# Last block: two chunks of the gated unit ahead of the last readout, and eight smaller moves on TensorE, ScalarE and VectorE

## The reference, cut to what matters

```python
def second_block(x, p, mix_norm, w_in, ...):
    xn = rms_norm_2(h, mix_norm[i])
    z = xn @ w_in[i]
    q, k, v, gate_a, u, gate_s = jnp.split(z, splits, axis=-1)
    attn = dilated_mixture_attention(q, k, v, ...) * jax.nn.silu(gate_a)
    ssm = s5_glu(u, ...) * jax.nn.silu(gate_s)
    h = h + jnp.concatenate([attn, ssm], axis=-1) @ w_out[i]
    gate = jax.nn.sigmoid(rms_norm_2(h, ple_norm[i]) @ w_ple_gate[i])
    h = h + gate * (p[i] @ w_ple_proj[i])
```

## Time and profile before

| what | value |
|---|---|
| median of 3 runs | 1368.23 us (1367.81 to 1368.30) |
| the profiled execution, its own time | 1368.63 us |
| its span, first to last instruction | 1366.9 us |
| mean granted TensorE clock | 0.999 |
| TensorE matmul busy | 1344.7 us (98%) |
| VectorE busy | 1020.6 us (75%) |
| ScalarE busy | 791.3 us (58%) |
| chain that ended last | TensorE 84%, VectorE 11%, ScalarE 3% |

### The profile page before, as it was taken

The page is one execution under the profiler, slowest core; times in us unless marked ns, Lnnn a source line. Parts: engine busy times, 40 slices in busy tenths (PEclk is TensorE's granted clock), DMA queues, the critical chain, the costliest instruction groups (busy, mean ns, idle before and its releaser), DMA issues.

```text
span 1366.9 us, 20597 instructions
## 1 busy us (share of the span) xinstructions
PE 1344.7 (98%) x6811; PEld 1105.3 (81%) x6811; DVE 1020.6 (75%) x1930; ACT 791.3 (58%) x1546; POOL 177.0 (13%) x323
## 2 busy tenths in 40 slices
PE   7999999999999999999999999999999999999998
PEld 6888888889987888889888888888888888887657
DVE  6978666669666766669766666699887777889986
ACT  6676555456555645558656554567665555675444
POOL 4100000000111000002000000001049993000000
PEclk9999999999999999999999999999999999999999
DMA  8534767775533767783336677745356766554132
GB/s 282 166 124 128 241 215 217 220 240 184 162 103 113 245 217 216 229 253 110 124 96 220 215 223 232 244 147 177 124 173 216 226 223 230 169 175 131 66 123 93
DMA packets 180310, 249.24 MB, mean 182 GB/s; under 512 B 10393, under 2 KB 124641, under 8 KB 180241
## 3 DMA queue, kind: packets, MB, share of 16 engines
q1 hardware_dynamic: 152352, 224.05, 50.7%
q10 hardware_dynamic: 25920, 18.89, 4.6%
q0 software_dynamic: 1968, 5.43, 1.4%
HBM read 237.84 MB, written 10.49 MB: 182 GB/s over the span
## 4 chain that ended last, share of the span: by engine, by line
PE 84%; DVE 11%; ACT 3%; issue 1%; DMA 1%; ACTq 0%; SPq 0%; DVEq 0%
PE ps L2112 21%; PE ps L2114 21%; PE ps L2113 21%; DVE w_rest L1382 3%; PE ps L2118 3%; PE ps L2126 3%; PE ps L2122 3%; ACT w_head L830 1%; PE ps L2448 1%; DVE x L1445 1%; PE ps L2933 1%; PE ps L2934 1%; PE ps L2935 1%; PE ps L2142 1%; PE ps L2965 1%
## 5 line engine op out<-in xcount | busy, mean ns | idle before, releaser
L2112 PE MATMUL ps<-w_head,xt_head 128*128 128x512 f32 (+1 forms) x1152 | 448.0, 389 | 3.3 <-DVE w_rest L1382 2.9
L2114 PE MATMUL ps<-w_head,xt_rest 128*128 128x512 f32 (+1 forms) x1152 | 441.5, 383 | 0.0
L2113 PE MATMUL ps<-w_rest,xt_head 128*128 128x512 f32 (+1 forms) x1152 | 441.0, 383 | 0.0
L830 ACT ACTIVATE w_head<-w_raw,gain_t 128x512 fp32r<-128x512 f32 (+1 forms) x596 | 375.1, 699 | 84.3 <-PE ps L2114 24.1
L1382 DVE SCALAR_TENSOR_TENSOR w_rest<-w_raw,gain_t,w_head 128x512 fp32r<-128x512 f32 (+1 forms) x596 | 417.3, 764 | 5.4 <-ACT w_head L830 4.7
L2112 PEld LDWEIGHTS ps<-w_head,xt_head 128*128 128x128 f32 x1152 | 217.2, 189 | 48.3 <-issue 6.4
L2114 PEld LDWEIGHTS ps<-w_head,xt_rest 128*128 128x128 f32 x1152 | 217.1, 188 | 42.9
L2113 PEld LDWEIGHTS ps<-w_rest,xt_head 128*128 128x128 f32 x1152 | 217.4, 189 | 39.8
L830 ACT ACTIVATE w_head<-w_raw 128x1024 fp32r<-128x1024 f32 x124 | 124.6, 1053 | 80.2 <-PE ps L2114 76.7
L1380 DVE TENSOR_TENSOR w_rest<-w_raw,w_head 128x1024 fp32r<-128x1024 f32 x124 | 146.8, 1222 | 6.6 <-ACT w_head L830 6.2
L1990 DVE SCALAR_TENSOR_TENSOR hid<-ps,rstd_x,gate_s 128x256 f32<-128x256 f32 x88 | 38.6, 480 | 119.3 <-ACT gate_s L1126 119.3
(11 more groups left out here) (502 smaller groups left out, 1699.1 us busy)
## 6 DMA issues: line engine op xcount, KB each, us to landing
w_raw<-in_ffn_w_gate_dram SPq DMA_DIRECT2D x88, 512.0 KB, 4.3
w_raw<-in_ffn_w_up_dram SPq DMA_DIRECT2D x88, 512.0 KB, 5.9
w_raw<-in_ffn_w_down_dram SPq DMA_DIRECT2D x88, 512.0 KB, 6.2
w_raw<-in_a_w_in_dram SPq DMA_DIRECT2D x48, 512.0 KB, 4.7
w_raw<-in_b_w_in_dram SPq DMA_DIRECT2D x24, 512.0 KB, 4.7
w_raw<-in_w_in_dram SPq DMA_DIRECT2D x24, 512.0 KB, 4.7
hid_way<-q_t ACTq DMA_DIRECT2D x36, 256.0 KB, 2.0
k_t<-hid_way ACTq DMA_DIRECT2D x144, 64.0 KB, 5.0
```

Source lines behind the costliest of these rows:

```text
L830: ins = act.activation(w_head[:, s, w], raw(u)[:, w], ACT.Copy, scale=1.0 if by is None else by)
L2112: pe.matmul(out_, hd, wh, start=first, stop=False)
L2113: pe.matmul(out_, hd, wr, start=False, stop=False)
L2114: return pe.matmul(out_, rt, wh, start=False, stop=last)
```

## The change

No instruction is added or taken out, and no operand changes. On TensorE, `half_unit(11, 1)` goes ahead of `readout(1)`; `weights_turned(2)` and `scores(3)` go ahead of `driven(6)` and `o_turn(0)`, and `readout(2)` ahead of `values(2)`; `o_turn(1)` goes between the two `out_a(1, (0, 1), m)`; and `glu(0)` and `glu(1)` go ahead of `readout(3)`. On ScalarE, `spread_out(1)` goes ahead of `proj_copied(0)` and `turned(gs_t[:, 0:2, :], 7)`, `spread_out(2)` ahead of `turned(gs_t[:, 2:4, :], 7)`, `head(u + OUT_S)` ahead of `gelu(3)`, and the second half of `head(u + OUT_S + 1)` behind the last `ssm_copied`. On VectorE, `gated(3)` goes into the middle of `turned_out(6)`. SyncE's and GpSimd's programs keep their order.

```diff
--- before.py
+++ after.py
@@ -1275,13 +1275,13 @@
                 spread_out(0)
                 exp(1)
                 out_of(5, gs_d, ACT.Silu)
+                spread_out(1)
                 proj_copied(0)
                 turned(gs_t[:, 0:2, :], 7)
-                spread_out(1)
                 exp(2)
                 proj_copied(1)
+                spread_out(2)
                 turned(gs_t[:, 2:4, :], 7)
-                spread_out(2)
                 o_copied(0)
                 exp(3)
                 spread_out(3)
@@ -1290,9 +1290,9 @@
                 gelu(1)
                 gelu(2)
                 o_copied(1)
+                head(u + OUT_S)
                 gelu(3)
-                head(u + OUT_S)
-                head(u + OUT_S + 1)
+                head(u + OUT_S + 1, some=(0, 2))
                 gate(0)
                 gate(1)
                 ssm_copied(0)
@@ -1301,6 +1301,7 @@
                 gate(3)
                 ssm_copied(2)
                 ssm_copied(3)
+                head(u + OUT_S + 1, some=(2, 4))
                 u += OUT_S + 2
                 n["x"] += 4
                 n["bank"] += 2
@@ -1607,7 +1608,7 @@
                     dve.wait_ge(bu_taken, h + 1)
                     step(dve.tensor_tensor(z1, z1, t_, ALU.subtract))
 
-                def turned_out(h):
+                def turned_out(h, between=None):
                     g, half = h // 2, h % 2
                     cs, sn = half_tiles(g, half)
                     t_, z0, z1, e_ = s5_piece[h]
@@ -1618,6 +1619,8 @@
                     step(last)
                     dve.tensor_tensor(t_, z0, cs, ALU.mult)
                     step(dve.scalar_tensor_tensor(e_, z1, -1.0, sn, ALU.mult, ALU.mult))
+                    if between:
+                        between()
                     dve.tensor_tensor(z0, z0, sn, ALU.mult)
                     dve.tensor_tensor(z1, z1, cs, ALU.mult).then_inc(xs_done, 1)
 
@@ -1698,8 +1701,7 @@
                 turned_in(6)
                 gated(2)
                 y_out(2)
-                turned_out(6)
-                gated(3)
+                turned_out(6, lambda: gated(3))
                 turned_in(7)
                 ssm_part(0)
                 turned_out(7)
@@ -2532,8 +2534,8 @@
                 pe.wait_ge(in_out, 8)
                 pe.wait_ge(turn_used, tr + 7)
                 values(0)
+                half_unit(11, 1)
                 readout(1)
-                half_unit(11, 1)
                 weights_turned(1)
                 pe.wait_ge(in_out, 12)
                 project(0)
@@ -2547,15 +2549,15 @@
                 project(1).then_inc(unit_used, 1)
                 pe.wait_ge(o_done_v, n["o_v"] + 2)
                 turn_group(gs_d, 1, 7)
+                weights_turned(2)
                 driven(6)
-                weights_turned(2)
+                pe.wait_ge(t_done, pair + 3)
+                scores(3)
                 pe.wait_ge(turn_used, tr + 9)
                 o_turn(0)
-                pe.wait_ge(t_done, pair + 3)
-                scores(3)
+                readout(2)
                 pe.wait_ge(o_there, 1)
                 values(2)
-                readout(2)
                 weights_turned(3)
                 pe.wait_ge(proj_out, 2 * M)
                 for m in range(M):
@@ -2563,9 +2565,9 @@
                 driven(7)
                 pe.wait_ge(o_done_v, n["o_v"] + 3)
                 values(3)
-                for m in range(M):
-                    out_a(1, (0, 1), m)
+                out_a(1, (0, 1), 0)
                 o_turn(1)
+                out_a(1, (0, 1), 1)
                 pe.wait_ge(o_there, 2)
                 for m in range(M):
                     last = out_a(0, (2, 3), m)
@@ -2574,10 +2576,11 @@
                     last = out_a(1, (2, 3), m)
                 last.then_inc(unit_used, 1)
                 pe.wait_ge(bu_taken, 8)
+                glu(0)
+                glu(1)
                 readout(3)
-                for k in range(4):
-                    last = glu(k)
-                last.then_inc(unit_used, 1)
+                glu(2)
+                glu(3).then_inc(unit_used, 1)
                 out_s_both(0)
                 there, base = xs(), n["xt"]
```

## The result

The median of 17 runs is 1372.43 us (1368.62 to 1374.35), against 1368.23 (1367.70 to 1368.70) before. The ratio is 1.0028, with a 95% interval of 1.0021 to 1.0034: slower by 4.2 us, 1.5 us above the end of the range. What the median hides is that the 17 executions are of two kinds. Before, all lay within 1.0 us. Now five have a mean granted TensorE clock of 1.000 and take 1368.62 to 1370.51, mean 1369.4. The other twelve have 0.996 to 0.998 and take 1371.77 to 1374.35, mean 1373.1. The profiled execution is of the second kind: 1373.14, span 1371.4, clock 0.996.

A forecast was written before the change was run, and what follows sets the result against it. TensorE, busy 98% of the span, was taken to bound the kernel. Waits going (3.0 us) against waits coming (4.4) and a tail count of 1.1 to 1.2 more gave 1369.4 us, range 1367.0 to 1370.9.

The forecast's parts named there:

- The chain of lateness: `readout(1)` behind the half unit delays VectorE 1.8 us at `turned_in(4)`; TensorE then waits 2.1 before `gs_d`'s second transpose.
- The wait for `exp(2)`: Before `weights_turned(2)` on TensorE: 0.7 us more of waiting, the transpose ending at 1293.1 against `exp(2)` at 1293.8.
- ScalarE's heads: Before `gelu(3)`: cost nothing while their loads are there; 0.3 to 0.4 us late at the longest landing, 0.4 kept for range.
- TensorE through the middle: From `project(0)` to the first `out_a`: new waits of 2.1 and 0.7 us, `out_a` starting at 1302.0, 1.4 late.
- rival (c): TensorE's clock falls during the new waits of 2.1 and 0.7; twelve slower matmuls cost 2.3 us, 1371.7; chance 0.07.
- (a): VectorE's delay does not reach TensorE; the 2.1 falls to 0.25 and only the tail is paid: 1367.5 us; chance 0.13.
- (b): Every wait of TensorE goes and none comes, the tail's included: -3.0, or 1365.2 us; chance 0.05.
- (d): `gated(3)` misses `o_turn(1)`, so VectorE's 1.8 comes through whole: 1370.1 us; chance 0.75 together with the forecast.
- the points that should prove the prediction wrong: No VectorE gap at `turned_in(4)`; `rest` ending before the first gate; 512-column matmuls behind the new waits starting over 0.4 apart.
- twelve matmuls near the start: After idling on loads in the earlier trace they took 5.20 us, 0.43 each, against 0.24 in a half unit.

The follow-up runs named there:

- the wait filled: The change with the second half of `project(1)` multiplied twice, four matmuls more before the second transpose of `gs_d`: 1369.21 us.
- the two variants that keep those waits: The change with `readout(3)` back ahead of all four `glu` chunks, 1372.54 us; the kernel before's change with only `rest(u + OUT_S)` moved ahead of `y_out(3)`, 1372.09 us.
- `glu` back: The change with `readout(3)` back ahead of all four chunks of the gated unit, the other moves kept: 1372.54 us, ratio 1.0027 to before.
- the longer wait: The kernel before with `half_unit(11, 1)` ahead of `readout(1)`, and the second transpose of `gs_d` also waiting for `exp(2)`: 1373.43 us.

## Why the prediction was wrong, point by point

**What held.** The chain of lateness came as it was worked out. VectorE stood still 1.87 before `turned_in(4)` (1.8 forecast), TensorE 1.97 before the transpose (2.1), 0.9 before `project(0)` (0.2 and 0.7 more), nothing before `readout(3)`, and 1.19 before `out_s_both(0)` (1.1 to 1.3). The wait for `exp(2)` was 0.44 and not 0.7, in an execution in which the clock was already falling; with the wait filled, where it did not fall, 0.56. ScalarE's heads cost nothing, as said: the first waits for its load, and `gelu(3)` still waits 1.67 for `y_out(3)` behind it, as ScalarE's timeline of the changed kernel shows:

```profile
1324.77 2.00 ACT L830 ACTIVATE w_head<-w_raw 128x1024 fp32r<-128x1024 f32 x2 [10.18 <-DMA w_raw<-in_w_out_dram]
1328.44 0.42 ACT L1238 ACTIVATE qkv<-qkv 128x256 f32<-128x256 f32 x1 [1.67 <-DVE qkv L1655]
```

The forecast of 1369.4 is the mean of the five executions without a fall, and the kernel with the wait filled, which did not fall in eleven executions, stands at 1369.21. As a sum of waits it was right.

**What failed.** The step that failed is the one in "TensorE through the middle" from the second transpose of `gs_d` to the first `out_a`. The sum has 9.4 there (0.7 and 8.7), with every matmul at the speed of the earlier trace rows, and puts the fall of the clock into rival (c) with a chance of 0.07. The profiled execution took 13.65 (1291.95 to 1305.60), 4.2 more, at a granted clock of 0.50 for most of it; with the wait filled the same stretch took 9.38 (1292.45 to 1301.83). Between 1264 and 1345 us no row of before had TensorE idle for longer than 0.86, so there was no evidence either way, and I treated that as evidence against. The fall came in 12 of 17 executions. Rivals (a), (b) and (d) did not come.

Of the points that should prove the prediction wrong, none came in its own words. The last asked for matmuls of 512 columns over 0.4 apart, and there is none of 512 columns in the slow stretch; the first ones, at 1305.60, ran at full speed again. Those of 384 columns show it: they start 0.32 apart (1297.13 and 1297.45), against 0.17 before (1295.07 and 1295.24).

**The price of (c).** It was sized at 2.3 from twelve matmuls near the start. The executions with a fall stand 3.7 above those without (1373.1 against 1369.4). In the profiled one, TensorE took 12.4 from `weights_turned(2)` to the first `out_a` (1293.16 to 1305.60), where the forecast had 8.2 (1293.8 to 1302.0): 4.2 more. What was mis-sized is the length of the slow stretch. The price took the twelve slow matmuls of the earlier trace rows; here the low level lasted for about ten us, nine of them without a gap in TensorE's work.

The Trainium skill, page "TensorE: Matmul & The Clock Gate", Part 1, names the slow clock as the default state, which activity lifts. The windows above agree for the loss: 1.00, then 0.50, after idleness, and no fall in the kernel where the idle time is filled. The same page of the Trainium skill says that the gate itself knows only these two levels; the windows between 0.50 and 1.00 here (0.59, 0.90) are those in which the level changes. The prediction named the first of the two and still gave its case the smallest chance but one.

## What to carry to other kernels

An order that moves a wait from several short ones into one long one on TensorE can lose more than the waits add up to: before such a move, find the longest single idleness that it makes, and put work that can go anywhere into it. When an instruction that another engine waits for is moved behind a filler, follow that engine's whole queue; here 0.9 us of saved wait was paid back as 2.0 some 18 us later. And where executions scatter by several us after a change and did not before, look at the granted clock of each before looking at the median.

## What the runs showed of the hardware that was not expected

The fall is not certain for a given program. With idle times of about 2.0 and 0.4 close together it came in 12 of 17 executions of the change, and in 17 of 21 of the two variants that keep those waits; with 2.6 in one piece in 4 of 5; with 1.4, and with 0.3 and 0.6, in none of 11 each. The 0.4 was not needed in the profile of the change. Its window from 1292 to 1293 reads 0.68, which puts the step from 1.00 to 0.50 at about 1292.4, and that wait began at 1292.7:

```profile
1292.00:1293.00 1.00, 0.72 (x4) 0.37 (x4) 1.00 (x3) 1.00 (x7) 0.00 (x0) 0.68 1.02 381
```

The length of the slow stretch is not fixed either. In the profile of the change it lasted from about 1292 to 1302 us; in those of `glu` back and of the longer wait it began after 1293 and was over soon after 1300 (the window from 1300 to 1302 reads 0.96 and 0.93), with TensorE busy for nearly all of it each time. What decides within one program whether the clock falls, and how long it stays low, these runs do not settle.
